# All down evictions of the second feed-forward by ScalarE and adding transfers

## The reference

```python
def swiglu(h, w_gate, w_up, w_down):
    return (jax.nn.silu(h @ w_gate) * (h @ w_up)) @ w_down
# per layer
x = x + g1 * y
x = x + g2 * swiglu(modulate(rmsnorm(x, norm_ffn[i]), sh2, sc2), ffn_w_gate[i], ffn_w_up[i], ffn_w_down[i])
```

## Time and profile before

| | |
|---|---|
| median of 3 runs | 2311.96 us |
| profiled execution | 2311.01 us |
| its span | 2309.7 us |
| TensorE busy | 2281.4 us, 99% |
| VectorE busy | 1691.9 us, 73% |
| ScalarE busy | 934.0 us, 40% |
| GpSimd busy | 245.3 us, 11% |
| far evictions and adding transfers | 144 each |
| near evictions by VectorE | 108 |

### The profile page before, as it was taken

The page is one execution under the profiler, slowest core; times in us unless marked ns, Lnnn a source line. Parts: engine busy times, 40 slices in busy tenths (PEclk is TensorE's granted clock), DMA queues, the critical chain, the costliest instruction groups (busy, mean ns, idle before and its releaser), DMA issues.

```text
span 2309.7 us, 29841 instructions
## 1 busy us (share of the span) xinstructions
PE 2281.4 (99%) x10881; PEld 1886.8 (82%) x10881; DVE 1691.9 (73%) x2580; ACT 934.0 (40%) x1549; POOL 245.3 (11%) x234
## 2 busy tenths in 40 slices
PE   8999999999999999999999999999999999999998
PEld 5888888888888888888888888888878888888887
DVE  5777788786688888888887762462897777777776
ACT  6355554562443222222222521111444555555554
POOL 0101101000300000000000300000301222222223
PEclk9999999999999999999999999999999999999999
DMA  8001111122212333333322011111103666666663
GB/s 302 35 26 54 44 52 43 43 99 103 64 37 73 110 110 108 102 110 110 110 101 92 19 56 36 55 55 37 55 16 76 130 130 129 130 129 129 130 152 92
DMA packets 72702, 201.15 MB, mean 87 GB/s; under 512 B 9856, under 2 KB 14336, under 8 KB 72448
## 3 DMA queue, kind: packets, MB, share of 16 engines
q1 hardware_dynamic: 51840, 161.72, 20.8%
q0 software_dynamic: 20736, 37.76, 10.0%
HBM read 157.51 MB, written 4.19 MB: 70 GB/s over the span
## 4 chain that ended last, share of the span: by engine, by line
PE 90%; DVE 6%; issue 1%; ACT 1%; DMA 1%; SPq 0%; POOL 0%; DVEq 0%; ACTq 0%; POOLq 0%
PE ps L790 25%; PE ps L792 24%; PE ps L791 24%; PE ps L1314 3%; PE ps L1248 2%; PE ps L1252 1%; PE ps L1250 1%; PE ps L1249 1%; PE ps L1253 1%; PE ps L1293 1%; PE ps L1294 1%; PE ps L1295 1%; DMA ada_ring<-ada_pe 1%; PE ps L1084 1%; DVE x L2687 1%
## 5 line engine op out<-in xcount | busy, mean ns | idle before, releaser
L2687 DVE SCALAR_TENSOR_TENSOR x<-ps,mods,x 128x512 f32<-128x512 f32 x296 | 214.7, 747 | 75.5 <-PE ps L792 55.8
L790 PE MATMUL ps<-h_hi,op_hi 128*128 128x512 f32 x640 | 249.3, 390 | 2.0 <-DVE op_lo L2511 1.1
L792 PE MATMUL ps<-h_hi,op_lo 128*128 128x512 f32 x640 | 249.0, 389 | 0.0
L2511 DVE TENSOR_TENSOR op_lo<-rq,op_hi 128x512 fp32r<-128x512 f32 x240 | 163.1, 687 | 67.3 <-ACT op_hi L2179 66.2
L790 PE MATMUL ps<-h_hi,w_hi 128*128 128x512 f32 x512 | 200.6, 392 | 1.6 <-DVE h_lo L2918 1.5
L790 PE MATMUL ps<-g_hi,w_hi 128*128 128x512 f32 x512 | 200.0, 391 | 0.0
L792 PE MATMUL ps<-h_hi,w_lo 128*128 128x512 f32 x512 | 199.3, 389 | 0.0
L791 PE MATMUL ps<-h_lo,w_hi 128*128 128x512 f32 x512 | 199.3, 389 | 0.0
L791 PE MATMUL ps<-g_lo,w_hi 128*128 128x512 f32 x512 | 199.2, 389 | 0.0
L792 PE MATMUL ps<-g_hi,w_lo 128*128 128x512 f32 x512 | 199.2, 389 | 0.0
L791 PE MATMUL ps<-h_lo,op_hi 128*128 128x512 f32 x480 | 186.7, 389 | 0.0
(11 more groups left out here) (442 smaller groups left out, 5425.0 us busy)
## 6 DMA issues: line engine op xcount, KB each, us to landing
rq<-stream SPq DMA_DIRECT2D x80, 512.0 KB, 4.0
x<-far POOLq DMA_DIRECT2D x144, 256.0 KB, 4.4
mod_raw_f<-ada_rows SPq DMA_DIRECT2D x48, 512.0 KB, 3.5
raw<-stream SPq DMA_DIRECT2D x46, 512.0 KB, 3.5
mod_raw<-ada_rows SPq DMA_DIRECT2D x32, 512.0 KB, 3.5
w_lo_f<-stream SPq DMA_DIRECT2D x28, 512.0 KB, 5.0
w_hi_f<-stream SPq DMA_DIRECT2D x18, 512.0 KB, 6.3
ada_ring<-ada_pe SPq DMA_DIRECT2D x16, 512.0 KB, 11.1
```

What stands on the lines that cost most here:

```text
L790: nc.tensor.matmul(out, w[0][wi], a[0][ai], start=start and not more, stop=False, skip_group_check=more)
L792: return nc.tensor.matmul(out, w[1][wi], a[0][ai], start=False, stop=stop, skip_group_check=more)
L2511: return nc.vector.tensor_tensor(dst, full, hi.bitcast(F32), ALU.subtract)
L2687: nc.vector.scalar_tensor_tensor(out=x[:, m, HALF[half]], in0=ps[:, out_bank(d, m), :], scalar=mods[:, gate + m:gate + m + 1], in1=x[:, m, ...
```

## The change

P7, P2 and P3 become far as well: `FAR = DOWNS`, `NEAR = ()`. The three calls of `near_out` in VectorE's stream go, and `far_out` calls come into ScalarE's. In ScalarE's first block three copies are placed earlier or later. In the last block VectorE's order of three `pair_lower` and `duo_lows` calls is another one. Waits that named VectorE's count `xe` now name `far_set` or `far_landed`.

```diff
-FAR = ("P1", "P6", "P4", "P5")
-NEAR = ("P7", "P2", "P3")
+FAR = DOWNS
+NEAR = ()
 def far_n(n, name, m):
-    return 16 * (n - 1) + 4 * FAR.index(name) + m
+    return 28 * (n - 1) + 4 * FAR.index(name) + m
...
 # down_read (TensorE)
-        if was in FAR:
-            eng.wait_ge(far_set, far_n(was_n, was, m) + 1)
-        else:
-            eng.wait_ge(xe, near_xe(was_n, was, m))
+        eng.wait_ge(far_set, far_n(was_n, was, m) + 1)
...
 # ScalarE, duo_first
             keep(0, GATE, "A11")
+            keep(0, UP, "A11")
             duo_tops(0, 4, 6)
             b_top("f1", "T1")
             pair_gate(0, "C11")
-            keep(0, UP, "A11")
             duo_tops(0, 6, 8)
-            pair_split(0, "C11")
             for n, (name, mat) in enumerate((("S2", GATE), ("S2", UP), ("S3", GATE), ("S3", UP))):
                 keep(0, mat, name)
                 duo_tops(0, n + 8, n + 9)
+                if n == 1:
+                    pair_split(0, "C11")
...
             duo_tops(1, 1, 2)
+            pair_gate(0, "C21")
             for what in ("T3", "C12", "T2"):
                 pair_split(0, what, True)
-            pair_gate(0, "C21")
...
 # ScalarE, duo_block
             duo_tops(n, 3, 4)
+            if n > 1:
+                far_out(n - 1, "P3")
             pair_split(n - 1, "T4", True)
...
             keep(n, GATE, "S2")
             duo_tops(n, 10, 11)
+            far_out(n, "P7")
             keep(n, UP, "S2")
...
-            duo_tops(n, 16, 18)
+            duo_tops(n, 16, 17)
+            far_out(n, "P2")
+            duo_tops(n, 17, 18)
...
 # ScalarE, duo_last
             keep(n, GATE, "S2")
+            far_out(n, "P7")
             duo_tops(n, 11, 12)
...
-            duo_tops(n, 14, 16)
+            duo_tops(n, 14, 15)
+            far_out(n, "P2")
+            duo_tops(n, 15, 16)
...
                 copy(w_hi[:, 4 + f, :], w_lo_f[:, 4 + f, :]).then_inc(dn_h, 1)
+            far_out(n, "P3")
             pair_gate(n, "C21")
...
             for m in range(4):
-                far_landed(act, n, "P5", m)
+                far_landed(act, n, "P3", m)
...
 # VectorE, duo_block (and the same three in duo_last)
-            near_out(n, "P7", gate)
...
-            near_out(n, "P2", gate)
...
-            near_out(n, "P3", gate)
...
 # GpSimd
-                    if name == "P5":
-                        pool.wait_ge(xe, near_xe(n, "P7", m))
+                    was = {"P1": "P2", "P6": "P3", "P7": "P5", "P4": "P4", "P2": "P1", "P5": "P7", "P3": "P6"}[name]
+                    if name in ("P2", "P5", "P3"):
+                        far_landed(pool, n, was, m)
                     elif n == 1:
                         pool.wait_ge(xe, xe_at(D_F1 + half, row))
-                    elif name == "P4":
-                        far_landed(pool, n - 1, "P4", m)
                     else:
-                        pool.wait_ge(xe, near_xe(n - 1, "P2" if name == "P1" else "P3", m))
+                        far_landed(pool, n - 1, was, m)
```

More of the change, by code:

```diff
@@ L442 @@
 PART = (slice(0, QT), slice(QT, HT))
-def near_xe(n, name, m):
-    return 8 * (D_F1 + 2) + 12 * (n - 1) + 4 * NEAR.index(name) + m + 1
 D_END = down_at(2 * WINO - 1) + 2
@@ L458, in xe_at @@
 def xe_at(d, m):
-    return near_xe(DUO_END, "P3", 3) + m + 1 if d == D_END else 8 * d + m + 1
+    return 8 * (D_F1 + 2) + m + 1 if d == D_END else 8 * d + m + 1
 def last_bank(m):
@@ L1659, in down_end_duo @@
                     if at == 0:
-                        pe.wait_ge(xe, near_xe(DUO_END, "P3", m))
+                        pe.wait_ge(far_set, far_n(DUO_END, "P3", m) + 1)
                     last = mm3(ps[:, 4 + m, :], (w_hi, w_lo), (ALL, 4 + at, slice(m * P, (m + 1) * P)),
@@ L2680, in to_x @@
             if d == D_END and m % 4 == 0:
-                for name in ("P4",) if m else ("P1",):
+                for name in ("P4",) if m else ("P2",):
                     for k in range(4):
@@ L3315, in pair_diff @@
             ins.then_inc(pair_sum, 1)
[L3317 to L3329, removed]
         def duo_first(gate):
@@ L3440, in duo_last @@
             duo_lows(n, 9, 10)
+            duo_lows(n, 10, 11)
             pair_lower(n - 1, "C12")
             pair_lower(n - 1, "C22")
-            duo_lows(n, 10, 11)
-            near_out(n, "P7", gate)
             duo_lows(n, 11, 12)
@@ L3492, in to_x_last @@
         def to_x_last(q, m):
-            if q == 0 and m == 4:
+            if q == 0 and m == 0:
                 for k in range(4):
-                    far_landed(dve, DUO_END, "P5", k)
+                    far_landed(dve, DUO_END, "P3", k)
             dve.wait_ge(dn_q, last_n(q, m))
```

## The result

The changed kernel takes 2358.4 us (median of 4 runs, 2355.07 to 2360.39), the kernel before beside it 2312.32 us: ratio 1.0201, interval 1.0189 to 1.0213, so 46.1 us slower. The forecast was 2312.3 with a range to 2320.0: 46 us too low, and 38 over the top of the range.

The account below looks back on a forecast made before the run. TensorE was taken as the bound, busy 2281.4 of 2309.7 us. First block -2.7, steady blocks +1.8 and last block +1.2 summed to +0.3, so 2312.3 us by the median; 8 in 10 range 2308.0 to 2320.0.

Parts of the forecast that it names:

- First block, -2.7: First block: three TensorE gaps worth 3.4 us go, a late low part of GATE S3 costs 0.7; gain 2.7 us.
- Steady blocks, +1.8: Blocks 1 to 8: P2's fourth eviction waits for P4's fourth landing, stalling P5 in three blocks; 1.8 us, bounds 0 and 12.
- the threshold was 44.24: Steady blocks: P4's fourth transfer stalls P5 if it lands over 44.24 us after the block's first product starts.
- 1.5 us later costs nothing: Steady blocks: DMA backlog delays w_hi_f by 1.5 us, within the 3.1 us of room at P1's operand; price 0.
- P6 lands near 24.2; 1.3 us of room: Steady blocks: P6 lands 24.2 us after the block's first product starts, so P7's evictions cause no 0.6 us stall at UP S3.
- 0.5 of room: Steady blocks: with P3 far, GATE S2's operand is ready by 15.8 us into the block against 16.32 due; no stall.
- The transfers, 0: Steady blocks: 28 adding transfers and the loads fill 54.5 of 57.1 us of DMA time; price 0, bounds 0 and 1 a block.
- Last block, +1.2: Last block: waits on far evictions at P4, P5 and P3 cost 2.4 us, less today's 1.2 gap; bounds -1.2 and +4.
- Rival (b): Steady blocks: far-buffer ring on ScalarE bounds P5's operand, each block losing 1.2 us; +7.8, 2319.8 us; chance 0.22.
- Rival (c): Steady blocks: w_hi_f loads starved beyond their room at P1, 1 us a block; +8.3, 2320.3 us; chance 0.06.
- (a): Steady and last blocks: nothing stalls, steady 0 and last block -1.2; total -3.9, 2308.1 us; chance 0.24.
- (d): Whole kernel: gain over 4.6 us, needing all four gaps to close without a new one; chance 0.03.

Follow-up runs that it names:

- e1: The kernel before with only the first block's three ScalarE copies moved; 2309.42 us, ratio 0.9995.
- e3: The kernel before with P2 alone made far as well in blocks 1 to 8; 2333.55 us, +21.5.
- e10: The kernel before with P2 alone made far as well in blocks 1 to 8, its evictions behind P5's cast; +6.5 us (1.0021 to 1.0052).
- e13: The kernel before with P2 far and P4 near in blocks 1 to 8; 2313.78 us, +2.7.
- e14: The changed kernel with only P7's evictions moved behind the keep of UP S2 and two casts; +34.7 us against the kernel before.
- e8: The kernel before with all seven down products far in the last block only; 2318.36 us, +6.3.
- e16: The changed kernel, P1's, P7's and P2's evictions later in blocks 1 to 8, transfers of P7, P2, P3 adding 64 of 512 columns; 2316.21 us, +5.2.

## Why the prediction was wrong, point by point

- **First block, -2.7.** Right in kind: the three gaps are gone, and one new one is there, on the low part of GATE S3, as said. By the starts it costs 1.6 us where I had 0.7, and the three cost 3.6 where I had 3.4, so the gain is 2.0; e1 gives 2.3 by its median. (Block 1 starts only 0.9 earlier in this profile; it is 1.1 late already at 1641, ahead of all edited work.) VectorE's sums, x additions and part of C11 ahead of that low part run 0.9 us later against the products than before; I had taken them as fixed. The trace shows what makes them late: the copy of UP A11, moved ahead of a cast, stands at the head of ScalarE's queue until TensorE has finished that product, and VectorE waits 0.84 us for the cast behind it, where the cast was done by 1709.9 before and VectorE did not wait. It is the same mistake on a small scale as in the steady blocks.

```profile
1712.87 0.59 ACT L2185 COPY pf_K<-ps 128x512 f32<-128x512 f32 x1 [10.34 <-PE ps L784]
1713.36 0.62 ACT L2171 CAST op_hi<-op_full 128x512 fp32r<-128x512 f32 x1
...
1714.01 0.69 DVE L2513 TENSOR_TENSOR op_lo<-op_full,op_hi 128x512 fp32r<-128x512 f32 x1 [0.84 <-ACT op_hi L2171]
...
1722.37 0.50 PE L782 MATMUL ps<-h_hi,op_hi 128*128 128x512 f32 x1 [1.35 <-DVE op_lo L2513]
```

- **Steady blocks, +1.8 against 39.2: the step that failed.** The landing was forecast well: 2050.36 (2042.86 + 7.5) is 48.3 us behind the block's first product (2002.11), or 43.7 with the 4.5 us taken off that the gaps in between cost, and the threshold was 44.24. The 2.0 us from landing to operand were right too: VectorE's `op_lo` of P5 ends at 2052.33, 0.6 us ahead of P5, which starts at 2052.96 without a gap. What failed is the sentence after it: "each landing later than 44.24 is a stall", and no other one costs. I took an eviction that waits as harmless when the next operand still comes in time. But the split of C22, the casts and the Silu of C12, VectorE's sums and the casts after them all go by turns between the two engines, and moved with P5's low part, 2.7 us later than before. At the end of the hand-over stand the loads of the next block. e3, e10 and e13 show by themselves what the wait ahead of P5's cast is worth: 21.5, 6.5 and 2.7 us.
- **"1.5 us later costs nothing" for w_hi_f.** I asked whether the loads get slower. They didn't (6.6 to 6.7 us). They were issued 2.7 us later, because SyncE waits for P3's low part, the end of that same chain. The 3.1 us of room at P1's operand held, since no gap is there on an operand; the room behind it, at the sums for GATE S2, UP S2 and P7, did not.
- **P7: "P6 lands near 24.2; 1.3 us of room".** It landed at T0 + 29.7 (2089.89 + 4.2 - 2064.44), because ScalarE reached P6's evictions not at T0 + 15.3 but at 20.4. I had credited VectorE's freed time to ScalarE, and left out that P3's and P1's evictions now wait for landings themselves. The stall of 0.6 that I had worked out and dismissed was there and cost 1.4. e14 prices it at 11.4 us.
- **P3: "0.5 of room" at GATE S2.** It was used up by P3's fourth wait (1.00) and P1's three (2.28). I had these evictions at 0.6 us pitch; here P1's follow one another at the pitch of the transfers before them, 1.4 and 1.6 us (2075.20, 2076.64, 2078.28).
- **The transfers, 0.** The sum was right (1.57 us each against 1.61). The fourth transfer took 4.2 us to landing in P6's group and 7.5 in P4's. The estimate of 2.6 us by the fit in the Trainium skill ("DMA: Bandwidth & Descriptors", "Anatomy of one DMA — SWDGE (gpsimd) path"), about 2.0 us and the bytes over 436e3, is far below both, so this case's traces do not agree with it. The w_hi_f loads took 6.7 us against 6.6, with 1.7 times the adding bytes in the block (7.32 against 4.20 MB). The Trainium skill has it that each DMA engine goes round its queues packet by packet (same page, "Queues, rings and completion order"); the slower loads that the prediction drew from it do not show here.
- **Last block, +1.2 against 10.8** (7.3 by itself in e8, 9.9 in the whole). The place was right: P2's evictions hold up P5's banks. The size was not: I gave 0.6 there. P4's fourth transfer, issued 0.2 us ahead of the two w_lo_f loads (2289.69), took 7.3 us instead of the ring's mean, and P2's fourth eviction waited 4.04 us for it:

```profile
2289.88 1.02 SPq L997 DMA_DIRECT2D w_lo_f<-stream  x2
```

```profile
2297.09 0.69 ACT L2217 ACTIVATE far<-ps,mods 128x512 f32<-128x512 f32 x1 [4.04 <-DMA x<-far]
```

```profile
2297.83 0.50 PE L782 MATMUL ps<-po_X,op_hi 128*128 128x512 f32 x1 [3.19 <-ACT far L2217]
```

  My bound of +4 added the loads by their sum; they came on one transfer. I had read the same thing in P4's steady landing, and not carried it over.
- **Rival (b)** named the mechanism, P2's wait for P4's landing, and the slower side, at 0.22. Its price used the same wrong step (one late operand a block), 1.2 us a block where 4.9 came. Rival (c) named the stretch (P1's weights) for a reason that did not hold. (a) and (d) fell.

Open: how the 39 us divide between the three groups. Singly they are worth 0.7, 21.5 and 2.0; by moves in the whole 11.4 for P7 and 15.1 for P2, and 5.1 for P1's (29.3 - 24.2), or 12 by the profiles. Open too: what an earlier issue of the w_hi_f loads alone would give back, and why P4's fourth transfer lands so much later than P6's. No version here beats the kernel before by more than can be measured; e1 is the nearest.

## What to carry to other kernels

When an instruction gains a wait on an in-order queue, don't stop at the first reader of what is behind it. Follow the lateness through the whole hand-over between the engines, to the next transfer whose issue depends on it, and once round the loop; a wait that reaches its own cause again is paid in every round. And a ring of buffers, each written again only when its transfer has landed, moves at the pitch of the landings, and one slow landing stops it: put such evictions behind the casts and copies that others wait for. In this case that gave back 29 of 46 us.

## Of the hardware, not expected

- Adding transfers of 256 KB hold the 16 DMA engines for 1.57 us each (71.1% of 61.90 us, 28 of them); the fourth of P6's group lands in 4.2 us, the fourth of P4's, issued close to the start of 512 KB loads, in 7.3 to 7.8 (after and e8).
- An adding transfer of an eighth of the columns (32 KB) still takes 2.4 us to landing, beside 4.8 for the whole ones in the same stretch (issue rows of e16, 2007.98 to 2065: KB each, median us to landing):

```profile
x<-far POOLq DMA_DIRECT2D x16, 256.0 KB, 4.8
x<-far POOLq DMA_DIRECT2D x12, 32.0 KB, 2.4
```

- After idle times of TensorE of 3.7 us (e8) and 4.4 us (e16), the granted clock was 0.51 and 0.50 in the 5 us behind, so a wait can be paid twice. The length of the last idle time alone does not decide it: after 3.2 us in the changed kernel the clock stayed at 1.00 (2298 to 2303), and after only 1.55 us in e14 (2272.66) it was at 0.56:

```profile
2272.66:2276.50 3.84, 3.84 (x10) 3.02 (x11) 1.39 (x2) 3.31 (x6) 2.36 (x4) 0.56 0.90 162
```
